# Modulation products of a diffusion layer pair on four column groups of TensorE, their first eight weight chunks through the expert buffers and the other sixteen in the last attention pair

## The reference, cut to what matters

```python
mod = jnp.einsum('bd,de->be', jax.nn.silu(cvec), lp['w_ada']) + lp['b_ada']
sh1, sc1, g1, sh2, sc2, g2 = [m[:, None, :] for m in jnp.split(mod, 6, axis=-1)]
h = rms_norm(x, lp['rms1_g']) * (1 + sc1) + sh1
u = h @ lp['w_in']                       # attention q, k, v; pooling; convolution
...
x = x + g1 * ((ga * y_a + gb * y_b + gc * y_c) @ lp['w_out'])
h2 = rms_norm(x, lp['rms2_g']) * (1 + sc2) + sh2
x = x + g2 * expert_choice_ffn(h2, ...)  # 16 experts, 3 matrices of 1024 x 1024 each
```

## Time and profile before

| | us |
|---|---|
| three runs | 3447.28, 3443.64, 3439.5 |
| median | 3443.64 |
| the profiled execution, its own time | 3443.1 |
| its span, first to last instruction | 3441.3 |
| PE busy | 3097.9 (90%) |
| DVE busy | 1981.0 (58%) |
| ACT busy | 1463.2 (43%) |

### The profile page before, as it was taken

How to read it: one execution, slowest core, us unless ns; L and a number is a source line. 1 busy time by engine, 2 the same in 40 slices (tenths; PEclk the granted TensorE clock), 3 DMA queues, 4 the chain that set the end, 5 groups by cost and what they waited for, 6 DMA issues and landing times.

```text
span 3441.3 us, 43751 instructions
## 1 busy us (share of the span) xinstructions
PE 3097.9 (90%) x17304; PEld 2395.2 (70%) x17304; DVE 1981.0 (58%) x1902; ACT 1463.2 (43%) x1586; POOL 465.2 (14%) x258
## 2 busy tenths in 40 slices
PE   5999998899995899999859999988999949999997
PEld 2978886588884566666529788866888835666664
DVE  2157767411125688988721577773111347888886
ACT  3223444311113577767532234443111236777774
POOL 0311111000000112122103111110000010222211
PEclk8998988899998899999989989998999979999998
DMA  6142221031114799999651422210211157999994
GB/s 215 65 137 67 73 76 38 0 115 63 62 55 176 270 379 368 375 371 373 235 194 64 136 70 72 80 34 31 87 62 62 56 212 282 371 372 372 370 378 170
DMA packets 275360, 601.13 MB, mean 175 GB/s; under 512 B 13648, under 2 KB 165360, under 8 KB 274448
## 3 DMA queue, kind: packets, MB, share of 16 engines
q1 hardware_dynamic: 261872, 549.09, 44.2%
q0 software_dynamic: 10272, 34.26, 3.8%
q10 hardware_dynamic: 3072, 15.73, 1.1%
HBM read 570.71 MB, written 28.31 MB: 174 GB/s over the span
## 4 chain that ended last, share of the span: by engine, by line
PE 83%; DVE 7%; DMA 3%; ACT 3%; issue 2%; POOL 1%; SPq 0%; DVEq 0%; ACTq 0%; PEldq 0%; POOLq 0%
PE ps L1261 20%; PE ps L1262 19%; PE ps L1263 19%; PE ps L1299 8%; PE ps L1312 2%; PE ps L1424 2%; PE ps L1400 2%; PE ps L1325 2%; DVE zc L944 2%; DMA raw<-in_w_ada 1%; DMA xg<-h_dram,next_token 1%; PE ps L1413 1%; PE ps L1342 1%; PE ps L1586 1%; DVE stats L974 1%
## 5 line engine op out<-in xcount | busy, mean ns | idle before, releaser
L1261 PE MATMUL ps<-h_hi,w_hi 128*128 128x320 f32 x1408 | 447.8, 318 | 74.0 <-DVE h_lo L899 46.4
L1176 DVE TENSOR_TENSOR m_lo<-m_raw_b,m_hi 128x2048 fp32r<-128x2048 f32 x192 | 439.4, 2289 | 73.3 <-ACT m_hi L786 70.9
L1176 DVE TENSOR_TENSOR m_lo<-m_raw_a,m_hi 128x2048 fp32r<-128x2048 f32 x192 | 438.8, 2288 | 69.7 <-ACT m_hi L786 67.6
L786 ACT CAST m_hi<-m_raw_b 128x2048 fp32r<-128x2048 f32 x192 | 367.1, 1912 | 179.0 <-PE ps L1263 179.0
L1262 PE MATMUL ps<-h_lo,w_hi 128*128 128x320 f32 x1408 | 440.8, 313 | 0.0
L1263 PE MATMUL ps<-h_hi,w_lo 128*128 128x320 f32 x1408 | 440.4, 313 | 0.0
L786 ACT CAST m_hi<-m_raw_a 128x2048 fp32r<-128x2048 f32 x192 | 366.4, 1911 | 164.5 <-PE ps L1263 161.5
L1261 PE MATMUL ps<-m_hi,xs_hi 128*80 128x512 f32 x1024 | 409.4, 400 | 3.3 <-DVE xs_lo L1191 3.3
L1262 PE MATMUL ps<-m_lo,xs_hi 128*80 128x512 f32 x1024 | 406.3, 397 | 0.0
L1263 PE MATMUL ps<-m_hi,xs_lo 128*80 128x512 f32 x1024 | 404.5, 395 | 0.0
L854 DVE TENSOR_TENSOR w_lo<-raw,w_hi 128x2048 fp32r<-128x2048 f32 x68 | 158.3, 2328 | 409.6 <-ACT w_hi L493 409.1
(11 more groups left out here) (249 smaller groups left out, 5028.3 us busy)
## 6 DMA issues: line engine op xcount, KB each, us to landing
m_raw_a<-in_w SPq DMA_DIRECT2D x192, 1024.0 KB, 7.2
m_raw_b<-in_w SPq DMA_DIRECT2D x192, 1024.0 KB, 7.3
raw<-in_w_ada SPq DMA_DIRECT2D x96, 512.0 KB, 4.6
raw<-in_w_in SPq DMA_DIRECT2D x72, 512.0 KB, 4.6
raw<-in_w_gate SPq DMA_DIRECT2D x48, 512.0 KB, 6.4
raw<-in_w_proj_a SPq DMA_DIRECT2D x16, 512.0 KB, 4.5
raw<-in_w_out SPq DMA_DIRECT2D x16, 512.0 KB, 4.7
x_dram<-x ACTq DMA_DIRECT2D x2, 2560.0 KB, 7.8
```

Source lines behind the costliest of these rows:

```text
L786: nc.scalar.copy(m_hi[:, n % RING], m_raw(slot)).then_inc(s["m_high"], 1)
L1176: nc.vector.tensor_tensor(m_lo[:, r], m_raw(slot), m_hi[:, r].bitcast(F32), ALU.subtract).then_inc(s["msplit"], 1)
L1261: pe.matmul(out, wh, xh, start=first, stop=False, skip_group_check=True)
```

## The change

All modulation products take one form, `ada(src, i, bank)`. A chunk is now 256 rows (two blocks of 128, `EK`) by 1024 columns of the matrix, still 1 MB, in rows of 4 KB instead of 1 KB. It takes 8 matmuls of 256 moving columns. The stationary operand is a window of 32 columns of a buffer of zeros that holds the two condition vectors (`csw`), and matmul q of four writes PSUM partitions 32q to 32q + 31, that is, another column group of the array. The window's position puts each 256-column piece in its own pair of output rows, so eight chunks accumulate to one PSUM bank of 128 x 256, which holds a third of the vector. ACT copies that bank (`ada_out`), PE sums and turns it with a constant matrix `fold` (`fold_ada`: two matmuls, 128 stationary columns, 16 moving), and DVE adds the bias (`add_mods`).

The first eight chunks of a layer go to the eight expert buffers. In the first layer they are loaded at the start of the kernel with no wait; in the second they are loaded as the last experts' buffers come free, and PE computes them (`ada_ring`) ahead of its wait for `ye`. `ada2`, the twelve narrow products and their `add_mods_of` are gone. The other sixteen chunks go through `raw[1]` and `raw[0]` in turn, in blocks 0 to 7 of the last pair, two in a block (`ada_raw`), with a wait for the buffer ahead of each.

```diff
             for l in range(DEPTH):
-                with seen.loop("ada1", 4) as i:
-                    for u in range(2):
-                        wide(u, ada_v[l, 2 * i + u])
                 for n, c0 in enumerate((POOL0, CONVB0, CONVA0)):
                     for u in range(2):
                         wide(u, in_v[l, c0 // CW + u])
-                with seen.loop("ada2", 2) as i:
-                    for u in range(2):
-                        wide(u, ada_v[l, 2 * i + u + 8])
...
+                for i in range(2 * RAWS):
+                    u = 1 - i % 2
+                    two = raw[:, u].rearrange("p (e q) n -> p e (q n)", e=EK)
+                    src = ada_chunk(l, 2 * FF, i)
+                    chunk(u, (two[:, 0], src[:, 0]), (two[:, 1], src[:, 1]))
...
-                seen("msplit", RAWS)
+                if l + 1 < DEPTH:
+                    for i in range(RAWS):
+                        sp.wait_ge(s["msplit"], seen("msplit"))
+                        seen.settle()
+                        sp.dma_start(m_raw(i), ada_chunk(l + 1, 0, i)).then_inc(s[f"mfull{i}"], 16)
+                else:
+                    seen("msplit", RAWS)
...
-            def ada(a):
...
-                for j in range(2):
-                    for k in range(KT):
-                        ins = pe.matmul(ada_at(a)[:, 2 * j:2 * j + 2], raw[:, 1, k, j * P:(j + 1) * P], cs[:, k, :], start=(k == 0), stop=(k == KT - 1))
+            def ada(src, i, bank):
+
+                c, k0 = i // 4, EK * (i % 4)
+                for e in range(EK):
+                    for q in range(4):
+                        a = 16 * (k0 + e) + 14 - 2 * (4 * c + q)
+                        ins = pe.matmul(ps[32 * q:32 * q + 32, bank, 0:CW], csw[:, a:a + 32], src[:, e, q * CW:(q + 1) * CW],
+                                        start=(i + e == 0), stop=(i == RAWS - 1 and e == EK - 1), skip_group_check=True)
+                return ins
+
+            def ada_ring():
+
+                for i in range(RAWS):
+                    pe.wait_ge(s[f"mfull{i}"], 16 * (25 * l + 1))
+                    ins = ada(m_raw(i), i, 6)
                 ins.then_inc(s["ada"], 1)
...
+            def ada_raw(i):
+
+                u = 1 - i % 2
+                pe.wait_ge(s[f"raw_full{u}"], seen(f"raw_full{u}", 32))
+                ins = ada(raw[:, u].rearrange("p (e q) n -> p e (q n)", e=EK), i % RAWS, 6 + i // RAWS)
+                if i % RAWS < RAWS - 1:
+                    ins.then_inc(s[f"raw_free{u}"], 1)
...
                 else:
+                    ada_ring()
+                    fold_ada(0)
                     pe.wait_ge(s["ye"], seen("ye"))
-                    ada_first()
                     turn_x()
                     sum_squares(KT, "sq")
...
+                        else:
+                            if i == 0:
+                                pe.wait_ge(s["dense"], 36 * (l + 1))
+                            if i < RAWS:
+                                ada_raw(2 * i)
+                            if i == 6:
+                                fold_ada(1)
+                            if i == 9:
+                                fold_ada(2)
                         turn_probs(g, i)
...
+                        if not more and i < RAWS:
+                            ada_raw(2 * i + 1)
                         values(g, i)
```

More of the change, by code:

```diff
@@ L535, in norm @@
                             h_high(k)
-            act.wait_ge(s["const_in"], 64)
-            nc.scalar.activation(cs[:], cs[:], ACT.Silu).then_inc(s["cs_ready"], 1)
+            act.wait_ge(s["const_in"], 80)
+            nc.scalar.activation(cs, c_in[:], ACT.Silu).then_inc(s["cs_ready"], 1)
             for l in range(DEPTH):
                 if l:
-                    ada_out(2, ada_row, 8)
+                    ada_out(0)
+                for i in range(RAWS):
+                    seen(f"mfull{i}", 16)
                 for k in range(KT):
@@ L676, in _ @@
                             value_out(g - 1, 2 * TT - 1)
+                        if not more and i == 5:
+                            ada_out(1)
+                        if not more and i == 9:
+                            ada_out(2)
                         if i in (2, 3, 4):
@@ L1316, in ada_used @@
-            def ada_used():
-                pe.wait_ge(s["ada"], seen("ada", 0))
-                pe.sem_inc(s["raw_free1"], 1)
-            def ada_wide(at, rslot):
-                pe.wait_ge(s[f"raw_full{rslot}"], seen(f"raw_full{rslot}", 32))
-                for k in range(KT):
-                    ins = pe.matmul(flat[0:2, bass.ds(at, CW)], cs[:, k, :], raw[:, rslot, k, :], start=(k == 0), stop=(k == KT - 1))
-                ins.then_inc(s["ada"], 1)
-                pe.wait_ge(s["ada"], seen("ada"))
-                pe.sem_inc(s[f"raw_free{rslot}"], 1)
@@ L1336, in turn_ada, with fold_ada @@
+            def fold_ada(n):
+                bank, at = ((7, 0), (6, CW), (7, CW))[n]
+                pe.wait_ge(s["ada_row"], 3 * l + n + 1)
+                for m in range(2):
+                    ins = pe.matmul(ps[:, bank, at + 16 * m:at + 16 * m + 16], ada_rows[n][:, m * P:(m + 1) * P], fold[:], start=True, stop=True)
                 ins.then_inc(s["ada_t"], 1)
@@ L1469, in _ @@
                 pe.wait_ge(s["z_ready"], seen("z_ready", 2))
-                with seen.loop("ada2", 2) as i:
-                    for u in range(2):
-                        ada_wide(CW * (2 * i + u) + 4 * 512, u)
                 for g in range(GROUPS):
@@ L1770, in constants @@
     tok[..., 1] = (np.arange(TT)[None, :] * P + np.arange(P)[:, None])[:, :, None]
-    return ident, cos, sin, cnt, slot, tok.reshape(P, TT, 2 * EXPERTS)
+    fold = np.zeros((P, 16), np.float32)
+    for r in range(16):
+        fold[r::32, r] = 1.0
+    return ident, cos, sin, cnt, slot, tok.reshape(P, TT, 2 * EXPERTS), fold
 def kernel(**inputs):
```

146 lines of the change are left out of this document (51 added, 95 removed).

## The result

The changed kernel takes 3321.7 us (3313.4 to 3333.1, four runs) where the kernel before takes 3443.7: a ratio of 0.965, 95% interval 0.962 to 0.968. It is 122 us faster. The forecast was 3275 (168 us faster), with a range of 3238 to 3330. The profiled execution took 3326.6 us.

What follows compares the result with a forecast made beforehand. PE, busy for 90% of the span, was taken as the bound. First layer 28 + 25 + 39 - 7 = 85 us saved, second 31 + 25 + 34 - 7 = 83: 3443 - 168 = 3275 us, range 3238 to 3330.

Steps and rivals of the forecast that it cites:

- The price of a chunk: Modulation products on PE: 0.9 us a chunk with four column groups at once, against 3.61 with no overlap; chance 0.70.
- by the prediction's estimate: Rival: matmuls overlap but no weight load does, so a chunk takes 3.0 us and the kernel 3361 us; chance 0.03.
- Head, layers, stage 3: Saved: 28 us at the first layer's head, 31 between layers, 25 in each layer's stage 3 and first tiles.
- Last pair: Sixteen chunks come in here and their loads decide: seven blocks grow by 1 us, 7 us lost in each layer.
- The round: A buffer's cycle in the last pair: matmuls 0.9, issue 0.8, landing 4.6, 6.3 us in all, against a 5.1 us block.
- Pairs 0 to 2: Each loses three narrow products: 13 us saved a pair, 8.5 at high clock; 39 us in layer one, 34 in two.
- 5 us of clock counted for five of six pairs: Part of the saving in pairs 0 to 2: a higher granted clock without the narrow products gives 5 us a pair.
- DVE's row of work: Waits the products covered in pairs 0 to 2 come open: 1.5 us in block 7, 2 in block 5.
- sign of error: Prediction is wrong if a chunk takes over 2 us, or DVE's or ACT's share of the chain grows in the pairs.
- Behind the last pair: The merge's own chunks load after block 7, covered by two blocks and the norms (50 us): no cost.
- Six pairs at 16 us: Upper bound of the saving in pairs 0 to 2; with last pairs free it gives 3243 us.
- the rival "slower": Rival: 32-column products run one after another at 1.2 GHz, 5.34 us a chunk, 3469 us in all; chance 0.03.

Runs made afterwards that it cites:

- one group: Changed kernel with all modulation products on column group 0, apart from the first four of each set of eight chunks: 3388.3 us, one run.
- two groups: Changed kernel with its modulation products on two column groups instead of four, the first four of a set as before: 3324.8 us, one run.
- four slots: Changed kernel with four buffers instead of two for the last pair's sixteen chunks, using the unused half of the split weights' buffers: 3296.4 us, ratio to before 0.955.
- edit of the taps: Changed kernel with five convolution taps of each of pairs 0 to 2 (blocks 5 and 7) done in the last pair, also called "taps late": 3289.2 us, ratio 0.952.
- four slots and taps: Changed kernel with four chunk buffers in the last pair and five taps of each of pairs 0 to 2 moved there: 3270.7 us, ratio 0.947.
- thin loads: Changed kernel with an eighth of each last-pair chunk loaded, all products kept, so the modulation is wrong: 3299.6 us, one run.
- the kernel before with the taps late: Kernel before the change, with the same five taps of pairs 0 to 2 done in its last pair: 3467.3 us, ratio 1.004.
- few products: Changed kernel with products of only 4 of the last pair's 16 chunks, the others still loaded, so the modulation is wrong: 3295.0 us, one run.
- the two kernels with spread chunks: Changed kernel with eight of the last pair's sixteen chunks moved into pairs 0 to 2: 3316.3 us; the same plus five taps moved to the last pair: 3279.2 us.

## Why the prediction was right, and where it missed

**The price of a chunk** was right: 0.94 us in the ring for 0.9, from the overlap of row groups in the earlier trace rows. Not luck: on one group it is 3.34 us, on two 1.72. The 2.38 times for three column groups in the Trainium skill ("TensorE: Matmul & The Clock Gate", Part 3) lies between the 1.9 times measured here for two groups and the 3.6 for four; no run here has three. The same part's rule, that a weight load overlaps a running matmul only where the row groups differ, would by the prediction's estimate have made a chunk 3.0 us. The trace doesn't agree: all four column groups use all rows, and a chunk with its 16 loads takes 0.94 us.

**Head, layers, stage 3** (109 forecast, 103 measured): right, with the late piece named in each. In the head it was ACT's wait for the second projection chunk behind 8 MB: it landed at 46.5 us (44.8 in the prediction), and ACT began to normalise at 48.3 instead of 46.5; between the layers, the tokens' reload with its landing of 8.65 us for the 8.9 of the earlier trace rows.

**Last pair.** The mechanism was right, two sizes were not. The round was put at 0.9 + 0.8 + 4.6 = 6.3 us; it measures 1.1 + 0.35 + 5.7 = 7.2. The landing of the earlier trace rows is a median over all transfers, and that median is 4.7 us here too; what binds is the later transfer of a chunk while the other slot loads, 5.7 us in the chain against the 4.64 of the earlier trace rows. That is 7 x 0.9 = 6 us a layer. And the round was set against a block of 5.1 us as if the products were inside it (the blocks 0 to 8 of that pair took 5.4 us on average). With four slots, where no load is late, the pair takes 59.2 us, so the products cost some 4 us whatever the loads do. In layer 1, where the granted clock is 0.88 instead of 0.94, 7 us more are lost. With four slots both layers take 59.2 and 59.3 us, so they hang on the round as well; the chain of layer 1 has one landing of 8.67 us (from 2144.41) and two of 6.8 and 7.1. Why these took so long is open.

**Pairs 0 to 2.** The two middle pairs of layer 0 and pair 1 of layer 1 gained 12.3 to 13.0 us, as forecast. The term that failed is the 5 us of clock counted for five of six pairs. Pair 0 has it in neither layer: it gave 8.7 and 9.5 us, and its granted clock is 0.91 before and after in layer 0, 0.90 and 0.92 in layer 1. (Before, its blocks 6, 8 and 9 were already 1.3 to 2.2 us shorter than those of pair 1.) And pair 2 of layer 1, where 8.5 was forecast for its high clock, gave 4.9: the clock fell from 0.98 to 0.96, and its block 6 grew from 7.5 to 8.2 us without its product. There what came to light was DVE's row of work, which the prediction had priced at 3.5 us a pair. The edit of the taps shows what it came to in the blocks 5 and 7 named there: 4.4 us in a middle pair. The prediction listed as a sign of error that DVE's share of the chain grows in the pairs; it did. By its own sign it was wrong there, though the middle pairs gave the 12 to 13 us forecast.

**Behind the last pair**, 11 us that the prediction counted as nothing. 7 of them are in the merge and the output projection (384.1 and 384.3 us for 380.6 in both layers before). The chain of the merge in the changed kernel (start, us, what):

```profile
751.42 5.33 issue
...
757.91 2.47 issue
```

The first of these is in the kernel before too (820.39, 5.34 us), the second is not. "issue" is time in which PE waited for nothing that the profile shows; this one stands three matmuls into the second turn of the merge's loop. In layer 0 it takes 2.5 us here and 2.1, 2.4, 2.7, 3.2 and 4.1 in the kernels with the taps late, four slots and taps, one group, four slots, and thin loads; in the kernel before with the taps late it is absent too. So it does not go with the last pair's length. But it is not in every form of the changed program: the kernel with few products has it in neither layer, and the two kernels with spread chunks have one stop of 8.7 and 9.0 us in layer 0 and none in layer 1.

The traces show what stands beside these stops: a few blocks of 16 KB of the kind "instruction" are loaded there. This is the account of the DMA queues for 747 to 765 us (packets, MB, share):

```profile
q8 instruction: 3, 0.05, 1.1%
```

In three of the 28 turns on record (14 kernels, two layers) no such block is loaded within 4 us before and 16 us behind the turn: layer 1 of the kernel with few products and of the two with spread chunks. There PE goes on after 0.9 us, and merge and output projection take 373.6 to 373.9 us. The turn in layer 1, in the changed kernel and in the one with few products:

```profile
2415.41 0.63 PE L1254 MATMUL ps<-h_hi,w_hi 128*128 128x320 f32 x1 [5.24 <-issue]
...
2419.49 0.42 PE L1254 MATMUL ps<-h_hi,w_hi 128*128 128x320 f32 x1 [2.92 <-issue]
```

```profile
2390.18 0.41 PE L1254 MATMUL ps<-h_hi,w_hi 128*128 128x320 f32 x1 [0.95 <-PE ps L1292]
```

So PE most likely waits there for its own program to be loaded, 5 us of it in the kernel before as well. That is read from what coincides and not tested, and why the blocks are loaded at one turn and not at another is open. Another 1.0 us is the squares behind the last pair of layer 0 (11.36 us for 10.32); the rest is spread.

**Slips in the prediction's own numbers**, none of which moves the forecast. Six pairs at 16 us are 23 us more than the 73 forecast and not 18, so the lower end is 3238 and not 3243; the range holds it. The rival "slower" took 5.34 us for a wide chunk at the low clock, "the one" of its kind. But the earlier trace rows has another of 5.30, and the clock was low for only 3.5 of the 5.34 us; a chunk wholly at 1.2 GHz would be some 7.2 us, an estimate as twice the 3.61 of the earlier trace rows. So this rival stood too low; it did not come.

The forecast was off by 47 us of 168, and the measured time lies 8 us inside the upper end of the range. That end stood for short gains in the pairs and slow last pairs, and both came in part. The 11 us behind the last pair were not in it; that they fitted in is luck.

## What to carry to other kernels

Price a load in a loop by the round of its buffer (products, issue, landing with the other buffers' loads beside it), and set that against the block with its new work inside. When the busiest engine loses work, the next engine's row between two handshakes becomes the block's length: look there for work that can move to a stretch which waits for something else (here 27 us in the six pairs for five taps each). And a faster matmul is worth little where its operand is late: with two slots, two column groups gave the same time as four. And compare two kernels stage by stage: two edits here looked 10 us better for a stop in the merge that they had nothing to do with.

## What the runs showed of the hardware

Four matmuls of 32 stationary columns on four column groups, each with all 128 rows, run at once in fp32: 0.94 us for 16 passes of 256 columns, 1.72 with two groups, 3.34 with one; and the order in which they are queued did not matter. The transfers of a last pair moved 274 GB/s with four slots and 237 with two, as means over a pair whose last blocks load little. Where the loads follow each other it was 342 GB/s with four slots (489 to 530 us, DMA share 0.95) and 302 with two (491.1 to 534.3 us, share 0.86), against the 407 of the earlier trace rows at a share of 1.02: a share of busy time is not a share of that rate. The second turn of the merge's loop cost PE 5.2 to 9.4 us of idle time in 25 of 28 cases, all with blocks of instructions loaded beside it, and 0.9 us in the three without.
